# Alternating long and short matmuls in the wide groups of a two-block transformer kernel

## The chip, the core and the metric

The kernel runs on one core of one Trainium2 chip. The time is the device time of one execution in microseconds. Three runs of the kernel before took 2044.04, 2044.32 and 2044.94 us, so the median is 2044.32 us.

## The reference

The reference applies two transformer blocks of two layers each to one sequence of 256 tokens with 1024 features, all in float32. The first block has two gated feed-forward parts per layer and between them a mixer of three branches (latent attention, differential attention, pooling). The second has another three-branch mixer and a squared-ReLU feed-forward part. Cut to the products that the change touches, each is a plain matrix product of the activations with a weight matrix, for example

```python
proj = x @ w_in                                   # the mixer's input projection
ff = jnp.square(jax.nn.relu(x @ w_ff1[l])) @ w_ff2[l]
```

## The kernel before, in words

Every weight matrix is streamed from memory in tiles of 1 MB. To keep nearly float32 accuracy at the matmul unit's faster number format, each weight tile is split in two: ScalarE writes a rounded high tile `wh` (line 1891), and VectorE writes the low tile `wl`, which is the raw tile minus the high one (line 2109). The activations are split in the same way into `xh` and `xl`, which lie side by side in the buffer `x2`: for each of the eight slices of 128 features, 256 columns of `xh` and then 256 columns of `xl`, one column per token. A product is the sum of three terms: high by high, low activations by high weights, and high activations by low weights.

Most products are done by the `tokens` items (line 1656): the activations are stationary in TensorE, 512 weight columns move past them, and there are three matmuls per slice. The `wide` items (lines 1660 to 1672) do it the other way round. There the weights are stationary. One matmul with the high weight tile moves all 512 columns of `x2`, so it does two of the three terms at once and puts them side by side in one bank of PSUM; one matmul with the low weight tile moves only the 256 columns of `xh` and adds to the bank's first half. In this text the first kind is called a long matmul and the second a short one. A wide item covers 128 output features: eight long matmuls, one per slice, and then eight short ones, 16 in all, into one bank. VectorE afterwards adds the two halves of the bank.

A planner, the class Plan, writes one list of items before the program is built; `pe_program` goes through it and emits TensorE's instructions in that order. Three waits stand ahead of each wide item: for the low tile, for the activations, and for the bank to have been emptied. The high tile is older than the low one, so no wait stands between the two loops. The last short matmul tells the other engines that the item is done. Each matmul instruction is preceded in the profile by a load of its 128 x 128 stationary operand, which runs beside the matmul ahead of it.

Of the kernel before, what the change touches and what calls it, by code (L numbers as in the profile page):

```python
# [1622 lines left out]
def pe_program(e, m, plan):  # L1623
# [4 lines left out]
    for it in plan.items:  # L1628
# [31 lines left out]
        elif k == "wide":  # L1660
# [5 lines left out]
            for s in range(8):  # L1666
                e.matmul(bank[:, :], hi[:, s, c], m.x2[:, s, :, :].rearrange("p a s -> p (a s)"), start=(s == 0),  # L1667
                         stop=False, skip_group_check=True)
            for s in range(8):
                ins = e.matmul(bank[:, 0:S], lo[:, s, c], m.xh[:, s, :], start=False, stop=(s == 7),  # L1670
                               skip_group_check=True)
            ins.then_inc(m.pe_done, 1)
# [829 lines left out]
def build(nc, A, out):  # L2502
    with ExitStack() as ctx:
        m = Memory(nc, A, out, ctx)
        plan = Plan(len(Plan(10 ** 9).units))
        m.units = plan.units
        block = ctx.enter_context(nc.Block())

        @block.sync
        def _(e):  # L2510
            sp_program(e, m, plan)

        @block.gpsimd
        def _(e):
            pool_program(e, m, plan)

        @block.scalar
        def _(e):
            act_program(e, m, plan)

        @block.vector
        def _(e):
            dve_program(e, m, plan)

        @block.tensor
        def _(e):
            pe_program(e, m, plan)
# [15 lines left out]
```

## Time and profile before

| what | value |
|---|---|
| median of three runs | 2044.32 us |
| span of the profiled execution, first to last instruction | 2042.5 us |
| TensorE matmul busy | 2034.5 us, 100% of the span |
| TensorE weight loads busy | 1718.3 us, 84% |
| VectorE busy | 1389.1 us, 68% |
| ScalarE busy | 1018.4 us, 50% |
| long matmuls of wide items (line 1667) | 1568, in 196 items |
| short matmuls of wide items (line 1670) | 1568, in 196 items |

The span leaves out what lies around the first and the last instruction; the median of the runs is 1.8 us above it. Engines: PE is TensorE's matmul side, PEld its weight loads, DVE VectorE, ACT ScalarE, POOL GpSimd. Matmuls overlap in the record: each is shown for as long as it takes from its start to its modelled end, and the next one starts before that end. What a matmul costs is therefore the distance from its start to the start of the next, not its own length.

### The profile page before, as it was taken

To read this page: it belongs to the slowest core of one execution; us is meant where nothing else is said; L and a number is where in the kernel's file an instruction comes from. 1 tells how busy PE (TensorE), PEld (TensorE's weight loads), DVE (VectorE), ACT (ScalarE), POOL (GpSimd) and SP (SyncE) were. 2 spreads that over 40 slices of the span, in tenths; PEclk is the share of its full clock that TensorE was granted. 3 is DMA by queue.
4 is the path that set the end of the run, shared out by engine and by line. 5 is a ranking of instruction groups with operands and counts; after the bars stand their busy time and mean duration, and the time that the engine had idled before them with its cause. 6 is when DMAs were issued, how large, how long until landed. Compare 5 with 4: busy or idle time off the path is not lost.

```text
span 2042.5 us, 25162 instructions
## 1 busy us (share of the span) xinstructions
PE 2034.5 (100%) x10364; PEld 1718.3 (84%) x10364; DVE 1389.1 (68%) x1624; ACT 1018.4 (50%) x1290; POOL 92.8 (5%) x133
## 2 busy tenths in 40 slices
PE   9999999999999999999999999999999999999998
PEld 7888888888888888888888888888888888888887
DVE  6655687775757566877675667757767677577675
ACT  6444576453445335775443365644444466445331
POOL 1001010000010001100100000000100000000000
PEclk9999999999999999999999999999999999999999
DMA  9655554465566656544656474555755656455552
GB/s 333 211 187 166 178 162 141 167 214 185 186 197 210 194 168 201 165 145 145 226 191 197 153 242 155 166 172 173 239 186 189 204 153 194 156 185 193 196 189 83
DMA packets 225569, 377.73 MB, mean 185 GB/s; under 512 B 6592, under 2 KB 113216, under 8 KB 225456
## 3 DMA queue, kind: packets, MB, share of 16 engines
q1 hardware_dynamic: 221472, 362.64, 54.1%
q0 software_dynamic: 3984, 13.49, 2.2%
q8 instruction: 82, 1.34, 0.3%
q14 instruction: 31, 0.25, 0.0%
HBM read 375.05 MB, written 1.05 MB: 184 GB/s over the span
## 4 chain that ended last, share of the span: by engine, by line
PE 98%; DVE 1%; ACT 0%; issue 0%; DVEq 0%; POOL 0%; ACTq 0%; POOLq 0%
PE pb L1656 63%; PE pb L1667 18%; PE pb L1670 9%; PE pb L1679 2%; PE pb L1725 1%; PE pb L1803 1%; DVE wl L2109 0%; PE pb L1802 0%; PE pb L1790 0%; PE pb L1860 0%; PE pb L1782 0%; PE pb L1645 0%; DVE lS L2292 0%; PE pb L1649 0%; PE pb L1647 0%; PE pb L1684 0%
## 5 line engine op out<-in xcount | busy, mean ns | idle before, releaser
L1891 ACT ACTIVATE wh<-raw 128x2048 fp32r<-128x2048 f32 (+2 forms) x347 | 654.2, 1886 | 626.6 <-PE pb L1656 271.3
L2109 DVE TENSOR_TENSOR wl<-raw,wh 128x2048 fp32r<-128x2048 f32 (+2 forms) x347 | 777.3, 2247 | 149.0 <-ACT wh L1891 147.8
L1656 PE MATMUL pb<-wh,x 128*128 128x512 f32 (+1 forms) x2144 | 651.3, 385 | 0.0
L1656 PEld LDWEIGHTS pb<-wh,x 128*128 128x128 f32 x2144 | 400.7, 188 | 77.9
L1656 PE MATMUL pb<-wl,x 128*128 128x512 f32 (+1 forms) x1072 | 421.1, 393 | 0.1
L1667 PE MATMUL pb<-x,wh 128*128 128x512 f32 x1568 | 397.0, 395 | 0.0
L1667 PEld LDWEIGHTS pb<-x,wh 128*128 128x128 f32 x1568 | 283.3, 189 | 51.8
L1656 PE MATMUL pb<-wl,mh 128*128 128x512 f32 (+1 forms) x740 | 255.7, 391 | 0.0
L1656 PE MATMUL pb<-wh,ml 128*128 128x512 f32 (+1 forms) x740 | 253.7, 388 | 0.0
L1656 PE MATMUL pb<-wh,mh 128*128 128x512 f32 (+1 forms) x740 | 253.5, 388 | 0.0
L1656 PEld LDWEIGHTS pb<-wl,x 128*128 128x128 f32 x1072 | 201.4, 188 | 42.2 <-issue 3.7
L1670 PEld LDWEIGHTS pb<-x,wl 128*128 128x128 f32 x1568 | 213.9, 190 | 15.4
L1670 PE MATMUL pb<-x,wl 128*128 128x256 f32 x1568 | 218.6, 282 | 0.0
L1656 PEld LDWEIGHTS pb<-wh,ml 128*128 128x128 f32 x740 | 138.9, 188 | 29.0
L1656 PEld LDWEIGHTS pb<-wh,mh 128*128 128x128 f32 x740 | 139.0, 188 | 28.3
L1656 PEld LDWEIGHTS pb<-wl,mh 128*128 128x128 f32 x740 | 138.0, 188 | 26.8
L2154 DVE SCALAR_TENSOR_TENSOR h<-pb,h 128x512 f32<-128x512 f32 x72 | 48.1, 686 | 84.3 <-PE pb L1656 84.3
L2128 DVE TENSOR_REDUCE sg<-pb 128x256 f32<-128x512 f32 x102 | 70.1, 688 | 39.5 <-PE pb L1670 39.3
L2128 DVE TENSOR_REDUCE mn<-pb 128x256 f32<-128x512 f32 x54 | 37.1, 688 | 50.2 <-PE pb L1670 50.1
L2149 DVE TENSOR_TENSOR ml<-pb,mh 128x512 fp32r<-128x512 f32 (+1 forms) x42 | 28.0, 675 | 45.2 <-ACT mh L1918 45.2
L1656 PE MATMUL pb<-wl,yph 128*128 128x512 f32 x128 | 51.5, 402 | 0.0
L1918 ACT ACTIVATE mh<-pb 128x512 fp32r<-128x512 f32 (+1 forms) x42 | 23.9, 582 | 54.2 <-PE pb L1679 54.2
(365 smaller groups left out, 1611.8 us busy)
## 6 DMA issues: line engine op xcount, KB each, us to landing
raw<-in_w_in_dram SPq DMA_DIRECT2D x100, 1024.0 KB, 5.3
raw<-in_w_ff_dram SPq DMA_DIRECT2D x64, 1024.0 KB, 5.3
raw<-in_ffn_w_down_dram SPq DMA_DIRECT2D x44, 1024.0 KB, 4.9
raw<-in_ffn_w_up_dram SPq DMA_DIRECT2D x42, 1024.0 KB, 5.3
raw<-in_ffn_w_gate_dram SPq DMA_DIRECT2D x41, 1024.0 KB, 5.3
raw<-in_w_branch_dram SPq DMA_DIRECT2D x24, 1024.0 KB, 5.0
raw<-in_w_out_dram SPq DMA_DIRECT2D x16, 1024.0 KB, 5.0
raw<-in_w_in_dram SPq DMA_DIRECT2D x4, 832.0 KB, 4.4
```

The lines of the kernel that those rows point to most:

```text
L1656: ins = e.matmul(pb[b][:, 0:c1 - c0], x[:, s, cols], w[:, n, c0:c1], start=(it["first"] and n == 0 and q == 0), stop=(it["stop"] and n == ...
L1667: e.matmul(bank[:, :], hi[:, s, c], m.x2[:, s, :, :].rearrange("p a s -> p (a s)"), start=(s == 0), stop=False, skip_group_check=True)
L1670: ins = e.matmul(bank[:, 0:S], lo[:, s, c], m.xh[:, s, :], start=False, stop=(s == 7), skip_group_check=True)
L1679: ins = e.transpose(bank[:, c * P:c * P + P], m.tile(it["src"], c), ident[:, :])
L1725: ins = e.transpose(bank[:, c * P:c * P + P], Sb[:, c * P:c * P + P], ident[:, :])
L1803: e.matmul(bank[:, 128:384], Q[0:w, P:S], key, start=True, stop=True).then_inc(m.pe_done, 1)
L1891: e.activation(hi, raw, ACT.Copy).then_inc(m.high_done, 1)
L1918: e.activation(hi, src, ACT.Copy).then_inc(m.turn_high, 1)
L2109: e.tensor_tensor(lo, raw, hi.bitcast(F32), ALU.subtract).then_inc(m.low_done, 1)
L2128: e.tensor_reduce(m.half(it["dst"], i), bank[:, :].rearrange("p (a s) -> p s a", a=2), AXX, ALU.add).then_inc(m.evac[use[0]], 1)
L2149: e.tensor_tensor(lo, src, hi.bitcast(F32), ALU.subtract).then_inc(m.evac[use[0]], 1)
L2154: e.scalar_tensor_tensor(o, bank[:, :], it["coef"], o, ALU.mult, ALU.add).then_inc(m.evac[use[0]], 1)
```

## The change

The second of the two loops is joined into the first. The eight long and eight short matmuls of a wide item are the same as before, with the same operands, the same bank, the same flags on the first and the last; now each long one is followed at once by the short one of the same slice. The waits ahead of the item and the signal behind it stay where they were.

```diff
             for s in range(8):
                 e.matmul(bank[:, :], hi[:, s, c], m.x2[:, s, :, :].rearrange("p a s -> p (a s)"), start=(s == 0),
                          stop=False, skip_group_check=True)
-            for s in range(8):
                 ins = e.matmul(bank[:, 0:S], lo[:, s, c], m.xh[:, s, :], start=False, stop=(s == 7),
                                skip_group_check=True)
             ins.then_inc(m.pe_done, 1)
```

On TensorE, at the first wide items of the first layer, the order before is this. `pb0` to `pb7` are the banks, `wh1_56` and `wl4_70` a high and a low weight tile, and x8 stands for eight such instructions in a row.

```order
L1656 MATMUL pb3<-wh0_55,x2_52 128x512 x2
L1667 MATMUL pb0<-x2_52,wh1_56 128x512 x8
L1670 MATMUL pb0<-x2_52,wl4_70 128x256 x8
L1679 MATMUL pb6<-ident_74,cn_128 128x128 x3
L1667 MATMUL pb2<-x2_52,wh1_56 128x512 x8
```

In the changed kernel the same place begins as follows, and goes on in the same way to the eighth pair.

```order
L1656 MATMUL pb3<-wh0_55,x2_52 128x512 x2
L1667 MATMUL pb0<-x2_52,wh1_56 128x512
L1669 MATMUL pb0<-x2_52,wl4_70 128x256
L1667 MATMUL pb0<-x2_52,wh1_56 128x512
L1669 MATMUL pb0<-x2_52,wl4_70 128x256
```

One passage from long to short per item has become eight, and line 1670 has become 1669, as has every later line by one.

The second place is on TensorE where one wide item follows another without anything between, from bank `pb2` to bank `pb1`. Before:

```order
L1667 MATMUL pb2<-x2_52,wh1_56 128x512 x8
L1670 MATMUL pb2<-x2_52,wl4_70 128x256 x8
L1667 MATMUL pb1<-x2_52,wh2_57 128x512 x8
L1670 MATMUL pb1<-x2_52,wl5_71 128x256 x8
L1694 MATMUL pb7<-pc_130,pin_126 128x256
```

In the changed kernel, around the passage from one bank to the other:

```order
L1667 MATMUL pb2<-x2_52,wh1_56 128x512
L1669 MATMUL pb2<-x2_52,wl4_70 128x256
L1667 MATMUL pb2<-x2_52,wh1_56 128x512
L1669 MATMUL pb2<-x2_52,wl4_70 128x256
L1667 MATMUL pb1<-x2_52,wh2_57 128x512
L1669 MATMUL pb1<-x2_52,wl5_71 128x256
```

The alternation runs on over the border of two items, since a wide item begins with a long matmul and ends with a short one. The orders of VectorE, ScalarE, GpSimd and SyncE hold the same instructions as before.

## Rows read from the trace of the kernel before

**Rows 1.** The page: busy time by engine; granted TensorE clock in 40 slices.
```profile
PE 2034.5 (100%) x10364; PEld 1718.3 (84%) x10364; DVE 1389.1 (68%) x1624; ACT 1018.4 (50%) x1290; POOL 92.8 (5%) x133
PEclk9999999999999999999999999999999999999999
```

**Rows 2.** Waits of TensorE: us in total, times, longest.
```profile
PE pb L1684 <- POOL fill L1564: 1.0, 1, 1.0
PE pb L1732 <- ACT lS L1982: 0.4, 2, 0.2
```

**Rows 3.** The page: chain that ended last, by engine, by line.
```profile
PE 98%; DVE 1%; ACT 0%; issue 0%; DVEq 0%; POOL 0%; ACTq 0%; POOLq 0%
PE pb L1656 63%; PE pb L1667 18%; PE pb L1670 9%; PE pb L1679 2%; PE pb L1725 1%; PE pb L1803 1%; DVE wl L2109 0%; PE pb L1802 0%; PE pb L1790 0%; PE pb L1860 0%; PE pb L1782 0%; PE pb L1645 0%; DVE lS L2292 0%; PE pb L1649 0%; PE pb L1647 0%; PE pb L1684 0%
```

**Rows 4.** Lines 1667 and 1670, whole span: ns min/median/max, first and last start.
```profile
L1667 PE MATMUL pb<-x,wh x1568: 387/392/586, 213.3 to 2001.7; 128*128 128x512 f32 x196
L1670 PEld LDWEIGHTS pb<-x,wl x1568: 187/192/192, 214.9 to 2002.7; 128*128 128x128 f32 x196
L1670 PE MATMUL pb<-x,wl x1568: 277/283/286, 215.1 to 2002.8; 128*128 128x256 f32 x196
```

**Rows 5.** Chain from 440 to 480: start us, us, what, count.
```profile
443.90 1.84 PE pb L1667 x8
445.74 0.95 PE pb L1670 x8
...
476.47 0.95 PE pb L1670 x8
477.42 2.75 PE pb L1656 x12
```

**Rows 6.** Chain from 1455 to 1500.
```profile
1464.68 32.67 PE pb L1656 x144
1497.35 1.81 PE pb L1667 x8
```

**Rows 7.** Groups of instructions, 213.40 to 214.80: busy us, mean ns.
```profile
L1667 PE MATMUL pb<-x,wh 128*128 128x512 f32 x7 | 1.7, 389 | 0.0
```

**Rows 8.** Groups, 219.21 to 219.42: last two shorts, first long.
```profile
L1670 PE MATMUL pb<-x,wl 128*128 128x256 f32 x2 | 0.4, 283 | 0.0
L1667 PE MATMUL pb<-x,wh 128*128 128x512 f32 x1 | 0.4, 396 | 0.0
```

**Rows 9.** Groups, 219.60 to 219.65: the second long.
```profile
L1667 PE MATMUL pb<-x,wh 128*128 128x512 f32 x1 | 0.4, 397 | 0.0
```

**Rows 10.** Groups, 219.60 to 220.80: the second to the seventh long.
```profile
L1667 PE MATMUL pb<-x,wh 128*128 128x512 f32 x6 | 1.5, 392 | 0.0
```

**Rows 11.** Groups, 221.11 to 221.14: the last long, the first short.
```profile
L1667 PE MATMUL pb<-x,wh 128*128 128x512 f32 x1 | 0.4, 389 | 0.0
L1670 PE MATMUL pb<-x,wl 128*128 128x256 f32 x1 | 0.3, 278 | 0.0
```

**Rows 12.** Timeline of TensorE, 219.21 to 221.3: start us, us, engine, what.
```profile
219.20 2.00 PE L1667 MATMUL pb<-x,wh 128*128 128x512 f32 x8
221.04 0.52 PE L1670 MATMUL pb<-x,wl 128*128 128x256 f32 x3
```

**Rows 13.** Timeline of weight loads at 221.12 and at 221.23.
```profile
221.04 0.19 PEld L1670 LDWEIGHTS pb<-x,wl 128*128 128x128 f32 x1
221.16 0.19 PEld L1670 LDWEIGHTS pb<-x,wl 128*128 128x128 f32 x1
```

**Rows 14.** Groups of weight loads, 221.17 to 221.20.
```profile
L1670 PEld LDWEIGHTS pb<-x,wl 128*128 128x128 f32 x2 | 0.3, 188 | 0.0
```

**Rows 15.** Line 1818, two 256-column matmuls between long ones: ns min/median/max.
```profile
L1818 PE MATMUL pb<-lrR,wguR x8: 278/284/289, 1274.4 to 1705.6; 128*128 128x256 f32 x8
```

**Rows 16.** Groups, 1274.83 to 1274.89: the long matmul behind line 1818's pair.
```profile
L1656 PE MATMUL pb<-wl,x 128*128 128x512 f32 x1 | 0.4, 401 | 0.0
```

## Prediction

> **What bounds the kernel now.** I read the busy shares first. TensorE's matmul side is busy for 2034.5 us of a span of 2042.5 us, and its granted clock is in the top tenth in all 40 slices, the level of 2.4 GHz [rows 1]; the reader is to see that nothing else comes near: VectorE has 68%, ScalarE 50%. A matmul's recorded length is modelled, so that share alone proves little; the waits do. TensorE waits for other engines for 1.0 us at the start and 0.4 us later, and for nothing else [rows 2]. The chain that ended last is 98% TensorE, with 18% of the span on line 1667 (the long matmuls) and 9% on line 1670 (the short ones) [rows 3]. So every nanosecond between two matmul starts is on the path, and the question is only at what distance the matmuls follow each other in the new order.
>
> Next come the distances. The clearest stretch is a row of wide items with nothing between them, where the chain goes from 443.90 to 477.42 in 12 items [rows 5]: 33.52 / 12 = 2.793 us an item, or 349 ns for one long and one short together. Long matmuls among long ones go faster: 144 of line 1656 take 32.67 us, 227 each, and the eight longs of an item right behind them take 1.81, 226 each, against 1.84 behind a wide item [rows 5, 6].
>
> For single matmuls I use their lengths. A settled long one is 389 ns long and starts 226 after the one before [rows 6, 7]. Settled short ones are 283 long [rows 8]. An item's shorts take 0.95 us for eight [rows 5], with the first of them shorter than the rest, so the settled distance is 120. Both differences are 163, and distance = length - 163 is the rule by which I read the other rows:
> - first long behind shorts: 396, so 233, which is 7 over settled [rows 8];
> - second long: 397, so 234, 8 over [rows 9]; second to seventh together: mean 392, 229, 3 over [rows 10];
> - first short behind longs: 278, so 115, 5 under settled [rows 11].
>
> The distances thus depend on the neighbour. Going to short gains 5 once; going to long costs 7 at once and some more over the next longs, which fades before the last long (389 again [rows 11]).
>
> **The change part by part.** It removes nothing and adds nothing: 1568 long and 1568 short matmuls with as many loads [rows 4], the same waits ahead of an item and the same signal behind its last short. The other engines' orders are unchanged. The signal comes at the end of the item in both orders, so ScalarE and VectorE, which use the freed tiles and the bank, see it earlier or later only by what TensorE itself gains or loses. DMA issues stay where they are. The low tile is waited for ahead of the whole item before and after, so the earlier first use of `wl` adds no wait. These edits cost nothing, and their cover is that no other engine bounds the kernel.
>
> What moves is neighbourhood. An item has now eight passages from long to short and eight from short to long (with the one over the border to the next item) in place of one each. So each short is a first short behind a long, and each long a first long behind a short. Taking the two rows for these at their word: 233 + 115 = 348 ns a pair, 8 x 348 = 2.784 us an item, against 2.793 measured. That is 9 ns an item, and over 196 items 1.8 us.
>
> How much does this depend on what the trace does not show, a long behind exactly one short and a short behind exactly one long? My reading of the rows is that a load beside a running matmul takes some of its time, part of which falls into the next matmul's distance: the first short behind longs is spared such a part from a load long finished, and the first long behind shorts gets one. In steady alternation what one is spared the other pays, so a pair should cost about the settled sum, 226 + 120 = 346, or up to the present mean. From below: if each long kept its settled 226 and each short its 115, a pair is 341. From above: the nearest row with few shorts between longs is line 1818, two 256-column matmuls of other tiles, whose lengths run from 278 to 289 [rows 15] and behind which the long is 401 [rows 16], so 126 and 238, or 364 a pair. I take 348, since it uses the same line's own rows on both sides of a passage.
>
> The bounds for the whole kernel, by (8 x pair - 2793) x 196 ns: 341 gives -65 an item or -12.7 us; 346 gives -25 or -4.9; 351 gives +15 or +2.9; 364 gives +119 or +23.3. Some items stand behind transposes or other small work (the longest long is 586 [rows 4]); since a long stays first there, what its start costs is the same in both orders.
>
> The profile's span is 2042.5 us, and the median of the runs 2044.32, 1.8 above it for what lies around the span. The change does not touch that. 2044.3 - 1.8 = 2042.5 us is my time.
>
> **A rule of the skill against the row.** The timeline has the load for the second short starting at 221.04, just when the first short starts, and the next load at 221.16 [rows 12, 13]. A load is thus one matmul ahead of its use, not two. The Trainium skill (TensorE: Matmul & The Clock Gate, "Step-by-step: what each phase is for") says that the engine's 64-deep window pulls weight loads ahead of matmuls in flight. If that reached over more than one matmul, alternation would gain much; that is the third rival below. This case's rows do not show it, as the load behind the first short did not start under the long.
>
> **The rivals.**
>
> *Faster: the late part belongs to runs of shorts.* In a settled run of shorts the load takes 192 ns (the median in [rows 4]); under the first short it is 188 [rows 14], as if the load were not held up yet. If the 7 ns of the first long come from loads held up by several shorts in a row, one short would not cause them: 226 + 115 = 341 a pair, -12.7 us, 2031.6 us. Against it: the shorts have a median of 283 [rows 4], and eight of them take 0.95 us [rows 5], which is 115 for the first and about 119 for each of the other seven; so the second short already has to pay, and with it, I think, a long in its place.
>
> *Slower: the disturbance carries over.* The second long behind shorts is 8 over settled although only a long precedes it [rows 9], and the six take 3 over in the mean [rows 10]. So a passage leaves something that fades over several matmuls. If the matmul behind each first long pays those 8 whatever its size, a short costs 115 + 8 = 123, and a pair 233 + 123 = 356: +55 an item, +10.8 us, 2055.1 us. The place is every short of line 1669, the price 8 ns each; it decides from a pair of 352 on, 4 over my own. Line 1818's neighbours speak for it, and would put it as high as 364 and 2067.6 us. Against it: the first short behind a disturbed long is not in these rows, and line 1818 reads other tiles.
>
> *Much faster: loads two matmuls ahead.* Then a short would have no load of its neighbour's to wait for. 256 more columns cost 226 - 120 = 106, so a short would cost about 106 and a pair 332: -137 an item, -26.9 us, 2017.4 us. The rows on loads speak against it.
>
> That the change does not do what it says is no rival here, as the order of TensorE's instructions shows the alternation.
>
> **How the numbers follow.** A change of less than 0.2%, 4.1 us, I count as none, which is about what a measurement of this kernel can tell. My forecast, a pair of 346 to 351, is 2039.4 to 2047.2 us, and nearly all of it within 0.2%; I give it 0.50. The first rival has 0.21 and the third 0.03, so faster has 0.24, and slower has 0.26 for the second rival. Since cases of both signs are near, the range goes to 2030 below (the first rival with a little room) and to 2056 above (the second rival at 356), and leaves out the third rival and line 1818's price.
>
> **What would show it.** In the profile of the changed kernel the row of 12 items between two `tokens` items should take some 33.4 us, 2.784 each. The lengths should be about 396 for the long matmuls and 278 for the short. Longs at 389 with shorts at 278 would show the first rival; shorts near 286 with longs at 396 or more, the second; shorts near 270, the third. The chain should stay 98% TensorE, and the waits of TensorE should stay at about 1 us. I am wrong if a pair lies under 346 or over 351, or if a wait of TensorE for another engine appears.

## The result, and the profile after

The changed kernel takes 2049.17 us (median of ten runs, 2048.82 to 2049.86) against 2044.35 us for the kernel before beside it (ten runs, 2043.94 to 2044.94). The ratio is 1.0024, with a 95% interval of 1.0016 to 1.0032: slower by 4.8 us. The forecast was 2042.5 us, no change; the range of 2030 to 2056 us holds the time, but the change is clear of the noise and goes the way of the second rival. One of the eleven executions of the version with runs of four, below, took 4138.36 us, with longer matmuls, and the ratio given there leaves it out.

The page of the changed kernel, its busy time by engine and its chain that ended last:

```profile
span 2047.5 us, 25162 instructions
PE 2039.1 (100%) x10364; PEld 1716.1 (84%) x10364; DVE 1389.7 (68%) x1624; ACT 1019.0 (50%) x1290; POOL 92.6 (5%) x133
PEclk9999999999999999999999999999999999999999
PE 98%; DVE 1%; DMA 0%; ACT 0%; issue 0%; DVEq 0%; ACTq 0%
```

TensorE's waits in the changed kernel (us in total, times, longest):

```profile
PE pb L1683 <- POOL fill L1564: 1.0, 1, 1.0
PE pb L1731 <- ACT lS L1981: 0.4, 2, 0.2
PE pb L1645 <- ACT wh L1890: 0.2, 1, 0.2
```

The span has grown by 5.0 us, from 2042.5 to 2047.5, and TensorE's busy time by 4.6. The granted clock is unchanged, the chain is 98% TensorE as in [rows 3], and the waits of TensorE are those of [rows 2] with 0.2 us more. So the loss lies in the spacing of matmuls. The groups of the page for the two kinds, with busy time and mean length in ns, first those of the kernel before (lines 1667 and 1670), then those of the changed one:

```profile
L1667 PE MATMUL pb<-x,wh 128*128 128x512 f32 x1568 | 397.0, 395 | 0.0
L1670 PE MATMUL pb<-x,wl 128*128 128x256 f32 x1568 | 218.6, 282 | 0.0
L1667 PE MATMUL pb<-x,wh 128*128 128x512 f32 x1568 | 559.2, 401 | 0.0
L1669 PE MATMUL pb<-x,wl 128*128 128x256 f32 x1568 | 439.7, 280 | 0.0
```

The longs have become longer by 6 ns, the shorts shorter by 2. The busy times can't be compared, since they are those of stretches in which any matmul of the line is open.

For the row of items that the prediction used I take the 13 items between a group of transposes and the next long run of line 1656. The transposes in the chain of the kernel before:

```profile
440.66 0.44 PE pb L1679 x4
```

They end at 441.10, and line 1656 begins at 477.42 [rows 5]: 36.32 us. The same stretch in the chain of the changed kernel (start us, us, what, count), with a piece of its inside:

```profile
440.67 0.44 PE pb L1678 x4
...
460.54 0.23 PE pb L1667
460.77 0.12 PE pb L1669
460.89 0.24 PE pb L1667
...
461.60 0.23 PE pb L1667
...
476.79 0.24 PE pb L1667
...
477.85 2.33 PE pb L1656 x10
```

From 441.11 to 477.85 are 36.74 us, 0.42 more, or 32 ns an item. Over the whole kernel it is 5.0 us / 196 = 26 ns an item. The reader is to see the repetition: from 460.54 to 461.60 there are three pairs in 1.06 us, and from 460.89 to 476.79 fifteen times as much, 15.90 us. The order of the instructions repeats after every pair, the time only after three. The single lengths in that piece, from groups in three narrow windows of the changed kernel (at 460.62, 460.98 and 461.34):

```profile
L1667 PE MATMUL pb<-x,wh 128*128 128x512 f32 x1 | 0.4, 395 | 0.0
L1669 PE MATMUL pb<-x,wl 128*128 128x256 f32 x1 | 0.3, 281 | 0.0
L1667 PE MATMUL pb<-x,wh 128*128 128x512 f32 x1 | 0.4, 403 | 0.0
L1669 PE MATMUL pb<-x,wl 128*128 128x256 f32 x1 | 0.3, 284 | 0.0
L1667 PE MATMUL pb<-x,wh 128*128 128x512 f32 x1 | 0.4, 398 | 0.0
L1669 PE MATMUL pb<-x,wl 128*128 128x256 f32 x1 | 0.3, 277 | 0.0
```

Less 163 each, the distances are 232 + 118, 240 + 121 and 235 + 114: pairs of 350, 361 and 349 ns, 353.3 in the mean, where the kernel before has 349 and the settled lengths would give 226 + 120 = 346.

Not every stretch of the changed kernel runs like this, and that is the part of its trace most worth learning from. Another row of 13 items stands between the same neighbours further on, again behind four transposes and ahead of line 1656. In the kernel before it lasts from 626.00 to 662.32, again 36.32 us:

```profile
625.56 0.44 PE pb L1679 x4
...
662.32 1.84 PE pb L1656 x8
```

In the changed kernel:

```profile
626.82 0.44 PE pb L1678 x4
627.26 0.23 PE pb L1667
627.49 0.11 PE pb L1669
627.60 0.23 PE pb L1667
627.84 0.12 PE pb L1669
...
663.32 1.84 PE pb L1656 x8
```

From 627.26 to 663.32 are 36.06 us, 0.26 less than before: 2.774 an item and 346.7 a pair, which is the settled sum. So one and the same order of instructions runs at 353.3 ns a pair in one row of 13 items and at 346.7 in another. The place does not decide it either. A row of three items takes 8.32 us in the changed kernel (1888.32 to 1896.64). The version with the short in the second half of the bank, an experiment below, has the same order, and there the same row takes 8.47 us (1888.22 to 1896.69). First the changed kernel, then that version:

```profile
1887.88 0.44 PE pb L1678 x4
...
1896.64 0.44 PE pb L1678 x4
```

```profile
1887.78 0.44 PE pb L1678 x4
...
1896.69 0.44 PE pb L1678 x4
```

Most rows of the changed kernel are of the dearer kind, and the cheaper ones are part of the reason why the mean over all items is 26 ns and not 32.

### The profile page after: what moved, and what is told of

It reads as the page before. It is cut to its first block, busy times and chain, and to the rows that moved or that the text cites. A ratio compares the mean times of both kernels' runs of the same rounds, so it can differ in the third digit from the quotient of the medians.

```text
span 2047.5 us, 25162 instructions
## 1 busy us (share of the span) xinstructions
PE 2039.1 (100%) x10364; PEld 1716.1 (84%) x10364; DVE 1389.7 (68%) x1624; ACT 1019.0 (50%) x1290; POOL 92.6 (5%) x133
## 4 chain that ended last, share of the span: by engine, by line
PE 98%; DVE 1%; DMA 0%; ACT 0%; issue 0%; DVEq 0%; ACTq 0%
PE pb L1656 63%; PE pb L1667 18%; PE pb L1669 9%; PE pb L1678 2%; PE pb L1724 1%; PE pb L1802 1%; DVE wl L2108 0%; PE pb L1801 0%; PE pb L1789 0%; PE pb L1859 0%; PE pb L1781 0%; PE pb L1649 0%; DVE lS L2291 0%; PE pb L1809 0%; PE pb L1717 0%; PE pb L1714 0%
## 5 line engine op out<-in xcount | busy, mean ns | idle before, releaser
L1667 PE MATMUL pb<-x,wh 128*128 128x512 f32 x1568 | 559.2, 401 | 0.0
L1669 PE MATMUL pb<-x,wl 128*128 128x256 f32 x1568 | 439.7, 280 | 0.0
L1667 PEld LDWEIGHTS pb<-x,wh 128*128 128x128 f32 x1568 | 294.6, 188 | 71.1
L1669 PEld LDWEIGHTS pb<-x,wl 128*128 128x128 f32 x1568 | 296.1, 189 | 0.8
L1656 PE MATMUL pb<-wh,ypl 128*128 128x512 f32 x128 | 50.0, 391 | 0.0
```

Of the source, the lines that this page charges most:

```text
L1656: ins = e.matmul(pb[b][:, 0:c1 - c0], x[:, s, cols], w[:, n, c0:c1], start=(it["first"] and n == 0 and q == 0), stop=(it["stop"] and n == ...
```

## The experiments

Theory A: a matmul's distance depends on the ones around it; equal lengths settle, unequal ones keep each other out of the settled state. Its rivals: a fixed price for each passage between lengths (B), a hold-up of the short because it adds to columns just written (C), a price for changing the weight tile (D). Later came F, on the length of the short, and E, on what the load takes.

**Runs of two.**

```diff
-            for s in range(8):  # eight pairs: long s, short s
+            for s0 in range(0, 8, 2):  # long s0, long s0+1, short s0, short s0+1
```

> Two long matmuls, then two short ones, four times an item. Theory A (each passage between unequal lengths puts the spacing of the matmuls out of its settled state, which takes some five equal matmuls to come back): the longs stay at about 233 and 236 ns, the shorts at 115 to 122, about 2.82 us an item, 2049 us, no better than full alternation. Theory B (a fixed price for each passage, 7 more passages an item cost 4.8 us): three more passages than before cost 2.1 us, 2046.4 us. Theory C (the short matmul adds to columns that the matmul just ahead has written, and is held up for it): half of the shorts follow a long, so about half of the loss, 2046.8 us.

2043.02 us beside 2044.17, ratio 0.9995 (0.9986 to 1.0004): not slower than before at all, and 6 us faster than full alternation. All three theories missed it. The same stretch in its chain:

```profile
440.22 0.44 PE pb L1680 x4
...
441.12 0.24 PE pb L1671 x2
441.36 0.47 PE pb L1668 x2
441.82 0.23 PE pb L1671 x2
442.05 0.46 PE pb L1668 x2
...
476.88 32.65 PE pb L1656 x144
```

From 440.66 to 476.88 are 36.22 us, 0.10 less than before. There are four times as many passages as in the kernel before, so a price for each passage (B) is out. The pieces alternate between two values, 0.47 + 0.23 and 0.46 + 0.23 or 0.24: this order, too, has a repeating row, but a cheaper one. The whole-span lengths of its short matmuls (ns min/median/max) show how:

```profile
L1671 PE MATMUL pb<-x,wl x1568: 274/277/285, 213.3 to 2001.2; 128*128 128x256 f32 x196
```

The median is 277, where [rows 4] has 283: at least half of the shorts are as cheap as a first one behind longs.

**Runs of four.**

```diff
-            for s in range(8):  # eight pairs: long s, short s
+            for s0 in range(0, 8, 4):  # four longs, then the four shorts of the same slices
```

> Four long matmuls, then four short ones, twice an item. Theory A: the row 233, 236, 228, 233 of the first four longs behind shorts, then 115 to 120 for the shorts, 930 + 472 = 1402 a half, 2.80 us an item, about 2046.5 us. Theory B: one more passage, +0.7 us, 2045.0 us. Theory C: two of sixteen matmuls follow a long of the same columns in place of one, 2045.0 us.

2046.10 us, ratio 1.0010 (1.0001 to 1.0019). A had 2046.5. One more run gave its trace:

> Four long matmuls, then four short ones, twice an item, once more for its profile: its median was 2046.1 us. Theory A as first put: 233, 236, 228, 233 for the longs, then 115 to 120 for the shorts. If each order has a repeating row of its own instead (as full alternation has 350, 361, 349 and runs of two 348.4 in the mean), the mean pair is (2046.1 - 2044.2) / 1568 us, 1.2 ns, over the 349.2 of before: 350.4.

2046.31 us. In the chain the row of 13 items lasts from 441.21 to 477.67, 36.46 us, or 2.805 an item and 350.6 a pair, near the 350.4 expected of it. So in this row the mean pair is 349 in runs of eight, 350.6 in runs of four, 348.3 in runs of two and 353.3 in runs of one. That does not rise with the number of passages. It goes with the idea that distances fall into repeating rows, and it stands against A as I first put it, in which two would have been as bad as one. Full alternation has at least two such rows, 353.3 and 346.7, so a row does not follow from the order alone.

**Mirrored items.** Every second item of a group does its shorts first.

```diff
+            if i % 2 == 0:
+                longs(True)
+                ins = shorts(False)
+            else:
+                shorts(True)
+                ins = longs(False)
```

> Every second item of a group does its shorts first, so that where items follow each other shorts meet shorts and longs meet longs; about half of the passages of the kernel before go. Theory A: a passage to longs and back costs some 20 ns net (27 for the longs, less 7 for the shorts), one saved per two items: about 2 us less than before, 2042.5 us. Theory B: half a passage saved an item at 0.1 us per 196 x 1/7: 0.4 us less, 2044.0 us. Theory C: no gain, 2044.4 us, since no passage ahead of an item costs anything.

2042.57 us (2042.13 to 2043.23) beside 2044.17 (2043.82 to 2045.05), ratio 0.9992 (0.9984 to 1.0001). The interval just reaches 1, though the two sets of runs do not overlap. Of the versions that do the same work it is the fastest, and near A's 2042.5 us. In its chain

```profile
440.77 0.44 PE pb L1691 x4
...
442.17 3.65 PE pb L1668 x16
...
477.40 2.72 PE pb L1656 x12
```

13 items take 36.19 us (441.21 to 477.40), 0.13 less than before. Sixteen longs take 3.65, where twice [rows 5] would be 3.68: the second eight go at the settled 1.81 of [rows 6].

**The short into the second half of the bank.**

```diff
-                ins = e.matmul(bank[:, 0:S], lo[:, s, c], m.xh[:, s, :], start=False, stop=(s == 7),
+                ins = e.matmul(bank[:, S:2 * S], lo[:, s, c], m.xh[:, s, :], start=False, stop=(s == 7),
```

> The alternation of the changed kernel, but the short matmul adds into the second half of the bank, which VectorE sums with the first anyway. Theory A and B: as the changed kernel, the cycle of 350, 361 and 349 ns a pair, 2049 us. Theory C: the short now writes the columns that the long has just written last, and the long begins with columns not touched since the long ahead, so distances change, by some ns a pair and several us in all.

2049.32 us, ratio 1.0024 (1.0014 to 1.0034), as the changed kernel. Which columns the short adds to does not matter; C is out. Runs of two say the same, since half of their shorts follow a long and the whole loses nothing.

**Equal lengths, in blocks and alternating.** The low tile's matmul moves all 512 columns, too.

```diff
-                ins = e.matmul(bank[:, 0:S], lo[:, s, c], m.xh[:, s, :], start=False, stop=(s == 7),
+                ins = e.matmul(bank[:, :], lo[:, s, c], m.x2[:, s, :, :].rearrange("p a s -> p (a s)"), start=False,
```

> The order of the kernel before, but the low tile's matmul moves all 512 columns, too, so that all 16 matmuls of an item have one length (the term low by low is added). Theory A: the spacing settles, 227 ns each, 16 x 227 = 3.63 us an item, about 2044.4 + 0.84 x 196 = 2209 us. Theory D (the price is that of going from one weight tile to the other, whose loads fall badly beside the moving data): one such change an item as before, 2209 us as well.

> Alternation of high and low tile as in the changed kernel, but all matmuls move 512 columns (the term low by low is added). Theory A: no lengths differ, nothing is disturbed, 227 ns each, the same 2209 us as the blocks of equal length. Theory D: sixteen changes of tile an item in place of two cost again, about 5 us more than the blocks of equal length, 2214 us.

Blocks: 2209.36 us, ratio 1.0808 (1.0790 to 1.0826). Alternating: 2209.16 us, 1.0807 (1.0791 to 1.0824). At 512 columns alternation costs nothing when the lengths are equal. The two lines in the alternating one, whole span, ns min/median/max:

```profile
L1667 PE MATMUL pb<-x,wh x1568: 387/390/583, 213.5 to 2167.5; 128*128 128x512 f32 x196
L1669 PE MATMUL pb<-x,wl x1568: 387/389/398, 213.8 to 2167.7; 128*128 128x512 f32 x196
```

Both settle at 389 to 390. Changing the weight tile at every matmul is free here, so D is out, and the price needs unequal lengths. Equal lengths are not enough by themselves, however. In the kernel before, line 1656 has rows of matmuls that all move 416 columns, and they do not settle. Two neighbours of such a row (window 193.83 to 193.90):

```profile
L1656 PE MATMUL pb<-wl,x 128*128 128x416 f32 x1 | 0.4, 357 | 0.0
L1656 PE MATMUL pb<-wh,x 128*128 128x416 f32 x1 | 0.3, 347 | 0.0
```

Over such a row the lengths run from 346 to 357 and repeat, where those of 512 columns in this experiment settle at 389 to 390.

**One weight tile for both.** The short matmul uses the high tile in place of the low one, so this version leaves out the term with the low tile and its product is another.

```diff
-                ins = e.matmul(bank[:, 0:S], lo[:, s, c], m.xh[:, s, :], start=False, stop=(s == 7),
+                ins = e.matmul(bank[:, 0:S], hi[:, s, c], m.xh[:, s, :], start=False, stop=(s == 7),
```

> Alternation as in the changed kernel, but the short matmul uses the high tile again, so that the term with the low tile is replaced by a second one with the high tile; sizes and loads are as before. Theory A: the lengths alternate still, so the cycle of 350, 361 and 349 ns stays, 2049 us. Theory D: both loads of a pair come from the same place, so the loss goes, 2044 us or less.

2049.42 us, ratio 1.0025 (1.0015 to 1.0035). The loss stays with both loads from one tile, which speaks against D as well.

**A short of 384 columns.**

```diff
-                ins = e.matmul(bank[:, 0:S], lo[:, s, c], m.xh[:, s, :], start=False, stop=(s == 7),
+                ins = e.matmul(bank[:, 0:384], lo[:, s, c], x2[:, 0:384], start=False, stop=(s == 7),
```

> Alternation as in the changed kernel, but the low tile's matmul moves 384 columns in place of 256 (half of the term low by low is added). Settled, such a matmul follows at 173 ns (line 1656 has some of that length in the kernel before) and a long one at 227, 400 a pair. Theory A: any two lengths that alternate stay out of the settled state, some 6 ns a pair over that sum, as 353 stands over 347: 406 a pair, 3.25 us an item, 2133 us. Theory F (only a short matmul that is about as long as a load disturbs the next): 400 a pair, 3.20 us an item, 2124 us.

2136.04 us in one run; A had 2133, F 2124. The chain of a piece of it:

```profile
540.15 0.23 PE pb L1668
540.39 0.17 PE pb L1670
...
541.78 0.23 PE pb L1668
```

Four pairs take 1.63 us (540.15 to 541.78), 407 each, 7 over the settled 400. With 256 columns the excess is 353.3 - 346 = 7, too. This order also has a second row: in three items behind transposes four pairs take 1.65 us (1521.14 to 1522.79), 413 each. How long a load holds TensorE can only be estimated. In the kernel before, line 1732 moves 64 columns a matmul, each with a load as long as those of the shorts (a median of 192 ns in the record), and two of them take 0.22 us:

```profile
282.97 0.22 PE pb L1732 x2
```

So a load holds TensorE for 0.11 us at most. A short of 384 columns, at 0.17 us, is clearly longer than that and disturbs as much, so F is out on that estimate.

**Half a load.** In the order of the kernel before, the low tile's load and matmul cover 64 of the 128 output features.

```diff
-                ins = e.matmul(bank[:, 0:S], lo[:, s, c], m.xh[:, s, :], start=False, stop=(s == 7),
+                ins = e.matmul(bank[0:64, 0:S], lo[:, s, i * P:i * P + 64], m.xh[:, s, :], start=False, stop=(s == 7),
```

> The order of the kernel before, but each low tile's load and matmul cover only the first 64 of the 128 output features (the rest of the term is left out); the columns moved stay 256. Theory A with the load beside a matmul as the source of what it takes over its columns' 107 ns: half a load takes half as much, the settled short goes from 120 to about 113 ns, 7 settled shorts an item, some 9 us less in all, 2035 us. Theory E (a fixed price for each matmul that has new weights, however long the load): 120 stays, 2044 us.

2037.17 us in one run beside 2044.30: 7.1 us less; A had 9. Line 1670 in its whole span, the loads and then the matmuls:

```profile
L1670 PEld LDWEIGHTS pb<-x,wl x1568: 133/134/136, 215.4 to 1995.5; 128*64 128x64 f32 x196
L1670 PE MATMUL pb<-x,wl x1568: 274/276/283, 215.6 to 1995.6; 128*64 128x256 f32 x196
```

The median short falls from 283 [rows 4] to 276, with the same 256 columns. 256 more columns cost 106 ns (226 - 120), so a settled short's 120 held some 14 ns beyond its columns; this version leaves some 7. E, a price that stays at 120, is out. That the load sets it is not shown: the edit halves the features that the matmul writes together with its load, and no run halves one alone. The first short behind longs (window 445.65 to 445.70) has even become longer, 281 for the 278 of [rows 11]:

```profile
L1670 PE MATMUL pb<-x,wl 128*64 128x256 f32 x1 | 0.3, 281 | 0.0
```

A load that simply takes its share of the matmul beside it does not explain that, since the load beside the last long was halved, too.

## Why the prediction was wrong, point by point

What bounds the kernel was right: only the spacing of matmuls moved the time, and no wait came or went that matters. That the edits themselves cost nothing was right as well; the clock, the waits and the runs with other columns and other tiles bear it out.

The step that failed is the one that took "the two rows for these at their word", 233 + 115 = 348, for every pair. The short of 115 ns was read behind a long that had settled, after seven others [rows 11], and the long of 233 behind a short that had settled [rows 8]. In most rows of the changed kernel no matmul follows a settled one. At 460 us its longs are at 232, 240 and 235, its shorts at 118, 121 and 114. The term for the long was too small by 2.7 in the mean (235.7 for 233) and the one for the short by 2.7 (117.7 for 115); 353.3 for 348 a pair is 8 x 5.3 = 42 ns an item, which turns the -9 of the sum into +33 and agrees with the 32 measured in the stretch. "In steady alternation what one is spared the other pays" failed there, too, since 353.3 is 7 over its 346. In the row from 627.26 it holds within a nanosecond, 346.7. So the prediction took for granted that the order of lengths sets the distances; the trace has two rows for one order, and most of the kernel fell into the dearer one. Nothing in the rows of the kernel before tells which one a stretch falls into.

The second rival came nearest: something is left behind by a passage and carries over, as the second long of [rows 9] showed, and it was to decide from a pair of 352 on. Its price was too high, 356 for 353.3, and its place was off: it laid the 8 ns on every short, while the runs show them on one long of three (240) and part of them on the shorts. For the row from 627.26 it does not hold at all. Its chance should have been larger: the six longs of [rows 10] had a mean of 229 for 226 although each had a long ahead of it, so the kernel before already showed that settling takes several equal matmuls, and the change leaves no two equal ones in a row.

The first rival (341 a pair) fell: single shorts do disturb the long behind them, and the cheaper row, too, is at 346.7. The third (loads two matmuls ahead, 332 a pair) fell, too: the shorts at 460 us are at 114 to 121, not at 106, and no row comes near 332 a pair. The bound from line 1818, 364, held, and its lone pair was the worst place to read a price from, as I said: the tiles and the neighbours are others.

Theory A had to be mended on the way. "Equal lengths settle, unequal ones keep each other out of the settled state" is shown for 512 columns in the wide items, which lose nothing in either order (2209.36 and 2209.16 us). As a general sentence it is not: 416 columns among their like do not settle, and alternating 512 and 256 columns run at the settled sum from 627.26 on. "The more passages, the worse" is not shown either: runs of two are cheaper than runs of four and eight. What stands is that distances fall into repeating rows, 346.7 to 353.3 a pair here, and that one order can have more than one of them. What sets a row, and which one a stretch falls into, was not settled: the transposes and the first long ahead of the two rows of 13 are the same instructions. Whether the load beside a matmul takes part of its time is argued from the half load and not shown.

## What to carry to other kernels

Where TensorE is the bound and every matmul has its own weights, the order of lengths is worth a trial, but a small one: mirroring the order in every second item gained 1.6 us by the medians here, with an interval that just reaches no change. A distance read behind a settled run does not hold where the order leaves nothing settled: before interleaving two kinds, look for how many matmuls a distance takes to settle after a change of length, and widen the range by the unsettled ones. A pattern's cost can't be had by counting its passages, so try two or three run lengths. And read more than one stretch of the trace: the same order can run at two prices in one execution, and a single stretch, however regular, speaks only for itself.

## What the runs showed of the hardware

- A settled 256-column matmul with a 128-column load beside it followed at 120 ns, some 14 more than its columns cost; with the load and the written features both halved some 7 more (283 and 276 ns of length; the loads themselves were 192 and 134 ns long). The Trainium skill (TensorE: Matmul & The Clock Gate, "Step-by-step: what each phase is for") says that "Loading the next tile's weights doesn't steal SBUF read bandwidth from the running matmul." No run here shows whether it does: none separates the load from the features written.
- A strictly periodic order of instructions can run with a longer period in time: alternating 512 and 256 columns repeated after three pairs, 1.06 us, some fifteen times without change.
- The same order can run at two steady prices in one execution: 353.3 ns a pair in the 13 items from 441.11 us, 346.7 in the 13 from 627.26.
- Equal lengths do not always settle: matmuls of 416 columns had lengths from 346 to 357 ns in a repeating row, those of 512 columns, alternating between two weight tiles, 389 to 390 in the median.
